# Two transformer blocks on one core: the ends of four stages computed in two halves of the positions

## What is computed

```python
mod = c_act @ mod_w[i] + mod_b[i]          # shifts, scales, gates; w_ada in block 2
y = mixer(rmsnorm(x, g_pre) * (1.0 + sc_m) + sh_m)    # ends in @ w2 (pw2), or @ w_out
x = x + gt_m * rmsnorm(y, g_post)          # "residual"
h = rmsnorm(x, g_pre_ffn) * (1.0 + sc_f) + sh_f       # "norm"
y = ffn(h)                                 # up products, gate, down products
x = x + gt_f * rmsnorm(y, g_post_ffn)
```

## Time and profile before

| | |
|---|---|
| median of 3 executions | 3444.75 us (3444.48 to 3445.12) |
| the profiled execution | 3445.46 us, span 3443.7 us |
| TensorE matmul busy | 3205.8 us, 93% |
| TensorE weight loads busy (beside the matmuls) | 2501.0 us, 73% |
| VectorE busy | 1513.4 us, 44% |
| ScalarE busy | 1024.8 us, 30% |
| GpSimd busy | 505.4 us, 15% |
| chain of work that ended last | PE 46%, DVE 4%, ACT 2%, DMA 1%, POOL 1% |
| mean granted TensorE clock | 0.954 |

### The profile page before, as it was taken

How to read it: one execution, slowest core, us unless ns; L and a number is a source line. 1 busy time by engine, 2 the same in 40 slices (tenths; PEclk the granted TensorE clock), 3 DMA queues, 4 the chain that set the end, 5 groups by cost and what they waited for, 6 DMA issues and landing times.

```text
span 3443.7 us, 33500 instructions
## 1 busy us (share of the span) xinstructions
PE 3205.8 (93%) x13818; PEld 2501.0 (73%) x13818; DVE 1513.4 (44%) x1620; ACT 1024.8 (30%) x1220; POOL 505.4 (15%) x210
## 2 busy tenths in 40 slices
PE   6897889999999999889999998899989999999996
PEld 1683456677888888668888877676666788888885
DVE  3777754353343344554521065577324422222225
ACT  2344435233222222233221132476222221111111
POOL 0397660100000000200200033000022000000002
PEclk8998998899999999979999999999999899999998
DMA  5113443302211211321332243531532121111112
GB/s 197 43 43 128 174 162 130 114 22 65 62 31 55 62 31 49 137 77 51 130 118 100 102 149 122 140 77 33 171 120 100 44 65 62 31 55 56 31 52 107
DMA packets 96191, 301.23 MB, mean 87 GB/s; under 512 B 11205, under 2 KB 15045, under 8 KB 95847
## 3 DMA queue, kind: packets, MB, share of 16 engines
q1 hardware_dynamic: 96040, 299.09, 26.5%
HBM read 251.34 MB, written 47.71 MB: 87 GB/s over the span
## 4 chain that ended last, share of the span: by engine, by line
PE 46%; DVE 4%; ACT 2%; issue 2%; DMA 1%; POOL 1%; SPq 0%; ACTq 0%; DVEq 0%; POOLq 0%
PE ps L651 38%; PE ps L697 2%; PE ps L988 2%; PE ps L1013 1%; PE ps L998 1%; DMA mainr<-sc_k 1%; PE ps L712 1%; DVE tmp L2044 1%; DVE tmp L2038 1%; POOL tmp L2277 1%; DVE tmp L2040 1%; DVE mainf L1672 1%; ACT mainr L1459 0%; PE ps L730 0%; DVE cols L2094 0%
## 5 line engine op out<-in xcount | busy, mean ns | idle before, releaser
L651 PE MATMUL ps<-mainr,wh 128*128 128x512 f32 (+1 forms) x7104 | 1939.9, 390 | 37.7 <-POOL wl L2205 11.6
L651 PEld LDWEIGHTS ps<-mainr,wh 128*128 128x128 f32 x7104 | 1337.4, 189 | 318.5 <-issue 40.9
L651 PE MATMUL ps<-mainr,wl 128*128 128x512 f32 (+1 forms) x3552 | 1131.5, 390 | 0.0
L651 PEld LDWEIGHTS ps<-mainr,wl 128*128 128x128 f32 x3552 | 671.8, 189 | 138.2
L1590 DVE TENSOR_TENSOR wl<-raw,wh 128x1024 fp32r<-128x1024 f32 (+2 forms) x256 | 271.1, 1063 | 630.2 <-ACT wh L1114 630.1
L1114 ACT CAST wh<-raw 128x1024 fp32r<-128x1024 f32 (+2 forms) x320 | 281.1, 886 | 749.5 <-PE ps L651 579.9
L2226 POOL TENSOR_TENSOR st<-st,tmp 128x1024 f32<-128x1024 f32 x24 | 57.5, 2396 | 1662.4 <-ACT tmp L1161 1662.1
L712 PE MATMUL ps<-raw,cols 128*1 128x512 f32 (+1 forms) x384 | 182.6, 632 | 43.7 <-DMA raw<-in_mod_w 18.3
L2205 POOL TENSOR_TENSOR wl<-raw,wh 128x1024 fp32r<-128x1024 f32 x64 | 154.3, 2419 | 456.0 <-ACT wh L1114 456.0
L697 PE MATMUL ps<-mainr,wh 128*128 128x512 f32 x576 | 164.6, 410 | 32.6 <-ACT mainr L1146 16.6
L1729 DVE TENSOR_TENSOR mainf<-mainf,ps 128x1024 f32<-128x1024 f32 x80 | 97.7, 1221 | 213.8 <-PE ps L651 213.0
(11 more groups left out here) (194 smaller groups left out, 2436.2 us busy)
## 6 DMA issues: line engine op xcount, KB each, us to landing
raw<-in_mod_w SPq DMA_DIRECT2D x48, 512.0 KB, 4.4
raw<-in_ada_w SPq DMA_DIRECT2D x48, 512.0 KB, 4.2
raw<-in_f_up SPq DMA_DIRECT2D x44, 512.0 KB, 3.5
raw<-in_g_up SPq DMA_DIRECT2D x44, 512.0 KB, 3.5
raw<-in_w_in SPq DMA_DIRECT2D x40, 512.0 KB, 4.1
raw<-in_pw SPq DMA_DIRECT2D x24, 512.0 KB, 3.8
sc_x<-mainf SPq DMA_DIRECT2D x24, 512.0 KB, 7.2
mainf<-sc_x SPq DMA_DIRECT2D x24, 512.0 KB, 7.5
```

What stands on the lines that cost most here:

```text
L651: ins = e.matmul(out, wt[:, a:b], xs[n], start=kk == 0 and t == 0, stop=kk == kt - 1 and t == 2)
```

## The change

The four ends are made in two halves of the positions, h = 0 (0 to 511) and h = 1. All eight tiles of the last product are made for half 0, then all eight for half 1. Each half has its own squares, four column sums (4 + 4 matmuls: all squares but the last are summed on GpSimd, then the last one apart), root, four diagonals, spread, residual and norm. While TensorE makes half 1's products, the other engines do half 0's residual and norm. Then the first three tiles of the next product are made in their half 0 and, after more of the end, in half 1.

- Weights: each weight of a last product is loaded and split twice, once per half (32 more loads, casts and low parts in all, half of them 512 wide). In the list, the next stage's first three weights now come before the eight pieces of modulation weights; before, they came behind them.
- PSUM: six half banks for the last products, one bank of statistics each for residual and norm; the temporaries are cut into ten halves.
- `tiles_abreast` takes the second and third tile one and three blocks behind the first, here and in the other two places that use it for full or half tiles (pw1, and the first tiles of pw2 and w_out).
- GpSimd: 6 adds of half width for each norm and half, 24 per end (12 in g's). Of g's residual it no longer does three adds.
- SP: the stores of x follow half 1's residual. The output is stored by halves.

The low part of a weight is now L1779 on VectorE, and a cast as before on ScalarE; columns L817, spread L824, modulation L772, turn L782, reciprocal L1848, diagonal L1854, residual L1863 and L1867, norm L1875, low part of it L1882, add of a last chunk L1929.

The core of the diff. Its pieces are, in this order: the table of what follows each end; the plan of an end (the list of weights, and the ring of half banks); TensorE's `tiles_abreast`, the end of pw2 and w_out (`project`), and that of f and g (`ffn_end`); the middle of ScalarE's `project`; VectorE's `project` and `ffn_end`; GpSimd's two. The functions they take the place of (`residual`, `square_columns`, `sums_added` and the like) are left out. `half_residual(s, i, h)` is a multiply and an add, `half_norm` and `half_lower` the norm's multiply and low part, `half_upper` its cast, `half_diagonal` a reciprocal and four diagonals.

```diff
...
+NEXT = {"pw2": ("n2", (3, 4), (("f_up", 0, 0), ("f_up", 0, 1), ("f_up", 1, 0))),
+        "f": ("n3", (5, 6), (("w_in", 0), ("w_in", 1), ("w_in", 2))),
+        "w_out": ("n4", (10, 11), (("g_up", 0, 0), ("g_up", 0, 1), ("g_up", 1, 0))),
+        "g": (None, (), ())}
...
+    def half_plan(self, s):
+
+        n, mods, first = NEXT[s]
+        for b in range(6):
+            self.bank.last[b] = self.acc.last[b // 2]
+        self.bank.only(*range(6))
+        for h in range(2):
+            for i in range(ND):
+                if s in ("f", "g"):
+                    key, src, done = (s + "_dn", LAST, i, h), self.d[f"{s}_dn{LAST}"][i], ("byadd", s, i, h)
+                else:
+                    key, src, done = (s, i, h), self.d[s][i], ("by", s, i, h)
+                self.weight(key, src, 128 * (len(CHUNKS[LAST]) if s in ("f", "g") else 8), "dve")
+                self.bank.take(key, done)
...
+        for key in first:
+            self.weight(key, self.d[key[0]][key[1] if len(key) == 2 else 2 * key[1] + key[2]], 1024, "dve")
+        for t, jb in enumerate(mods):
+            self.mod_weights("a", jb)
+            self.acc.put(2 - t, ("a", jb), *self.mod_free("a", jb))
...
+    def tiles_abreast(keys, kt, x, ready, outs, ends=True):
+
+        lags = (0, 1, 3)
+        for step in range(kt + lags[-1]):
+            for key, lag in zip(keys, lags):
+                kk, j = step - lag, k.W[key]
+                if not 0 <= kk < kt:
+                    continue
+                for event in ready(kk):
+                    w.wait_ge(*k.at(*event))
+                hi, lo = x(kk)
...
+        tiles_abreast([(s, i, 0) for i in range(3)], 8, part_of(x, 0), ready, lambda key: [k.BANK(*key)])
         for i in range(3, ND):
-            tile((s, i), 8, x, ready)
-        square_columns(s)
+            half_tile((s, i, 0), 8, x, ready, 0)
+        for i in range(ND):
+            half_tile((s, i, 1), 8, x, ready, 1)
+            if i == 0:
+                half_columns(s, 0)
+            if i == 1:
+                half_spread(s, 0)
+            if i == 5:
+                half_columns(n, 0)
+            if i == 6:
+                half_spread(n, 0)
+        modulation("a", mods[0], range(2))
+        half_columns(s, 1)
+        modulation("a", mods[0], range(2, 4))
+        half_spread(s, 1)
+        modulation("a", mods[1])
+        modulation_turn("a", mods[0])
+        first_tile(first[0], *following)
+        modulation_turn("a", mods[1])
+        half_columns(n, 1)
+        first_tile(first[1], *following)
+        half_spread(n, 1)
+        first_tile(first[2], *following)
+        x, ready = following
+        tiles_abreast(first, 8, part_of(x, 1), ready(1), lambda key: [k.ACC(*key)[:, 512:1024]])
...
+    def ffn_end(s, slots, following):
+
+        n, mods, first = NEXT[s]
+        fs = CHUNKS[LAST]
+        for h in range(2):
+            for i in range(ND):
+                half_tile((s + "_dn", LAST, i, h), len(fs), pairs(lambda kk: slots[0][fs[kk] % 5], lambda kk: slots[1][fs[kk] % 5]),
+                          lambda kk: [("uhi", s, fs[kk]), ("ulo", s, fs[kk])], h)
+                if (h, i) == (1, 1):
+                    half_columns(s, 0)
+                if (h, i) == (1, 2):
+                    half_spread(s, 0)
+        if not n:
+            half_columns(s, 1)
+            half_spread(s, 1)
+            return
+        modulation("a", mods[0])
+        half_columns(n, 0)
+        half_columns(s, 1)
+        modulation_turn("a", mods[0])
+        modulation("a", mods[1])
+        half_spread(n, 0)
+        half_spread(s, 1)
+        modulation_turn("a", mods[1])
+        x, ready = following
+        tiles_abreast(first, 8, part_of(x, 0), ready(0), lambda key: [k.ACC(*key)[:, 0:512]], ends=False)
+        half_columns(n, 1)
+        half_spread(n, 1)
+        tiles_abreast(first, 8, part_of(x, 1), ready(1), lambda key: [k.ACC(*key)[:, 512:1024]])
...
+        output(5, 1)
+        half_root(n, 0)
+        output(6, 1)
+        split_to(k.W[first[1]] + 1)
+        for i in range(7):
+            half_upper(n, i, 0, hi, shift, s, ND - 1)
+        output(7, 1)
+        split_to(k.W[first[2]] + 1)
+        half_upper(n, 7, 0, hi, shift, s, ND - 1)
...
+            split_to(k.W[s, i, 0] + 3)
+        split_to(k.W[s, 0, 1] + 3)
+        half_diagonal(s, 0)
...
+            half_residual(s, i, 0, y, x, x_load)
+            if i in (2, 5):
+                split_to(k.W[s, 1 + i // 3, 1] + 3)
+        split_to(k.W[s, 3, 1] + 3)
+        split_to(k.W[s, 4, 1] + 3)
+        half_diagonal(n, 0)
+        for i in range(ND):
+            half_norm(n, i, 0, x, s)
+            if i:
+                half_lower(n, i - 1, 0, hi, lo, shift, s, ND - 1)
+            if i in (1, 4):
+                split_to(k.W[first[i // 4]] + 1)
+        half_lower(n, ND - 1, 0, hi, lo, shift, s, ND - 1)
+        split_to(k.W[first[2]] + 1)
+        half_diagonal(s, 1)
+        for i in range(ND):
+            half_residual(s, i, 1, y, x, x_load)
...
+        def summed(i, h):
+            j = k.W[s + "_dn", LAST, i, h]
+            split_to(j + 3)
+            o = y(i)[:, 512 * h:512 * h + 512]
+            w.wait_ge(*k.at("tile", j))
+            w.wait_ge(*k.at("yadd", s, LAST - 1, i))
+            e.tensor_tensor(o, o, k.BANK(s + "_dn", LAST, i, h), ALU.add).then_inc(*k.to("byadd", s, i, h))
+
+        for i in range(ND):
+            summed(i, 0)
+        summed(0, 1)
+        summed(1, 1)
+        half_diagonal(s, 0)
+        summed(2, 1)
+        for i in range(ND):
+            half_residual(s, i, 0, y, x, x_load)
...
+        split_to(k.W[first[2]] + 1)
+        half_diagonal(n, 0)
+        half_diagonal(s, 1)
+        for i in range(ND):
+            half_norm(n, i, 0, x, s)
+            if i:
+                half_lower(n, i - 1, 0, hi, lo, shift, *last)
+            if i == 1:
+                modulation_add("a", mods[0])
+            if i == 4:
+                modulation_add("a", mods[1])
+        half_lower(n, ND - 1, 0, hi, lo, shift, *last)
+        for i in range(ND):
+            half_residual(s, i, 1, y, x, x_load)
...
+    def project(s):
+        n = NEXT[s][0]
+        squares_added(s, 0)
+        squares_added(s, 1, 1, 2)
+        squares_added(n, 0, 1, 3)
+        squares_added(s, 1, 2, 3)
+        squares_added(n, 0, 3, 7)
+        squares_added(s, 1, 3, 7)
+        squares_added(n, 1)
+
+    def ffn_end(s):
+        n = NEXT[s][0]
+        squares_added(s, 0)
+        squares_added(s, 1, 1, 3)
         for i in range(1, ND - 1):
-            w.wait_ge(*k.at("ysq", s, i))
-            if i > 1:
-                w.wait_ge(*k.at("yacc", s, i - 1))
-            e.tensor_tensor(k.S(0), k.S(0), k.TMP("ysq", s, i), ALU.add).then_inc(*k.to("yacc", s, i))
-
-    def sums_added(s):
-        for i in (1, 3, 5):
-            t = k.TMP("sum", s, i - 1)
-            w.wait_ge(*k.at("sumsq", s, i))
-            e.tensor_tensor(t, t, k.TMP("sum", s, i), ALU.add).then_inc(*k.to("sumadd", s, i))
+            if n:
+                squares_added(n, 0, i, i + 1)
+            if i + 2 < ND - 1:
+                squares_added(s, 1, i + 2, i + 3)
...
```

542 lines of the change are left out of this document (324 added, 218 removed).

## The result

The changed kernel takes 3454.24 us, the median of seven executions, against 3444.98 for the kernel before (3443.15 to 3446.5). One of the seven took 6466.14; the other six lie between 3450.6 and 3459.0, with a median of 3453.4. The ratio is 1.0026, 95% interval 1.0013 to 1.0038: slower by 9.3 us. The forecast was 3436, faster by 9. The time lies inside the range that was given, on the other side of no change.

A forecast was written before the change was run, and what follows sets the result against it. TensorE, busy 93% of the span, bounds the kernel; time can only come from its waits and non-product work. -10.3 + 2.7 - 11.9 - 2.0 + 13.1 - 4.0 + 3.2 = -9.2 gives 3436 us, range 3412 to 3458.

The forecast's parts named there:

- residual row of f's half 0 shared with GpSimd: At the f end: 4.6 us a row, 2.7 of it VectorE's own work, the rest for two GpSimd half adds.
- S: The moment in an end when TensorE starts the second half's products; later steps are timed from it.
- f end: End after f: half 0's chain outlasts half 1's products, 105.5 us against 92.4, so +13.1.
- weight (7,1) in pw2, w_out: At the pw2 and w_out ends: its low part stands behind half 0's norm, TensorE waits 5.0 us (2 to 8).
- g end: End after g: 51.4 us from S against 55.9 before, with a small allowance for GpSimd: -4.0 us.
- pw2 end: End after pw2: 58.7 us of work plus four waits and slow clock, 81.1 us against 91.4: -10.3.
- w_out: Its end 79.7 us against 91.6, -11.9; its start -2.0, as lags let more pieces run ahead of weight waits.
- Rival 3: At the ends GpSimd gets the port at every tie, residual rows of half 1 cost 2.6 us: 3456 us, chance 0.20.
- Rival 1: The f end comes out even because GpSimd's adds cost VectorE little: 3423 us, chance 0.17.
- Rival 2: At the ends only TensorE's own work counts, -30 us each, g -7.5: about 3345 us, chance 0.05.
- Rival 4: Even: the four waits near their upper ends in one of the pw2 and w_out ends, 3446 us, chance 0.13.
- The lags: At the starts of pw2 and w_out: pacing of the first three tiles changes, +2.7 us and -2.0 us.

The follow-up runs named there:

- experiment 2: The changed kernel with each load of x issued behind one weight of half 0, not all eight ahead of them, in all four ends: 3440.48 us.
- experiment 3: The changed kernel, but in f and g VectorE adds a half tile's product first and makes the low part behind it: 3450.80 us.
- experiment 4: The changed kernel with GpSimd's adds of squares cut to 8 of 512 columns, so the sums leave out most squares: 3428.85 us.
- experiment 6: The kernel before with only the lags of 0, 1 and 3 blocks in tiles_abreast, everything else as it was: 3420.49 us.
- kernel 1: The changed kernel, but the ring of three for high and low parts doesn't count an end's modulation weights, so the fourth weight takes the first tile's place: 3437.47 us.

## Why the prediction was right and wrong

**The step that failed** is one sentence: "The 32 more loads, casts and lower parts hide: ScalarE and VectorE are idle most of the product time". It was argued from idle engines. What counted was how long one weight lasts: 10.88 or 5.44 us of product before, 5.44 or 2.72 now, beside the queue ahead of it (the feed, 13.8 us in experiment 2) and the dependences from one weight to the next (the loop, 3.4 us in experiment 3). The sum had 0 for both, and the feed alone is enough to turn the sign: without it the kernel takes 3440.48, faster than before.

**The second, not in the sum at all,** is the place: the waits behind the third tile, 2.34, 0.91 and 2.94, of which the prediction says that each "stays". They became 5.05, 3.62 and 5.70, +8.2 us together by the rows, and 16.8 us when mended. The diff had it in view, the list of weights with the three ahead of the eight; I counted what that does to the loads, and not what it does to the ring that is indexed by the list.

**Term by term.**

| term | forecast | measured |
|---|---|---|
| residual row of f's half 0 shared with GpSimd | 4.6 | 4.55 |
| residual of f's half 0 ends, after S | 44.4 | 41.4 |
| third low part of w_in, after S | 47.3 | 44.3 |
| f end, from S | 127.3 | 122.8 |
| S in f, from the wait at the start of the chunk | 19.4 | 24.2 |
| weights (3,1), (4,1) in pw2 | 2 + 2 | 2.12 + 1.6 |
| weight (7,1) in pw2, w_out | 5.0 | 4.15, 4.05 |
| last modulation weight in pw2 | 2 | 2.51 |
| columns of half 1 in pw2 | 4 | 1.73 |
| g end: S, from the first product | 21.8 | 30.9 |
| g end from S | 51.4 | 53.8 |

The first row of the table is luck, as experiment 4 shows: GpSimd was taken at 1.9 us of a row and costs 0.67, and 1.21 is the wait for the cast that the sum left out.

The chain of the **f end** had the right owner, and its +13.1 came out as +13.5, but this is luck too, since several errors meet in it. S came 4.8 us late, which I put down to feed and loop without having taken it apart. From S on it was 4.5 shorter. The norm of half 0 began at S + 65.3, not 70. It took 11.1, not 14. The residual of half 1 took 12.8, not 15.5. What stands behind it took 33.7, not 27.8, and 2.8 of that is the longer wait of the place.

The **pw2 end**'s four waits were right in kind, three of them within 0.9 us; the stage is -1.2 and not -7.6, because of a feed wait of 3.32 and of 2.7 more behind the first tiles. **w_out** was -11.8 against -13.9, and the 2.7 more behind its first tiles would be enough for the difference. The **g end** was wrong in sign: its own chain was 2.4 longer than forecast, and S 9.1 late, by the wait of 4.63, the slow clock behind it, the loop, and a wait of 1.78 for the first half tile's input, which the kernel before does not have and which stays in experiment 2.

**The rivals.** Rival 3 said 3456 and named the port. The time is near its number by luck. Its mechanism was that a residual row of half 1 costs 2.6 us and not 1.94; in f three of these rows take 1.38 and five 1.71. GpSimd took less in the rows than the sum had for it, and it took something where the sum had nothing, in the half tiles of f and g. The place and the feed, 30.6 us when mended one by one, are none of the port; the loop, 3.4, is half of it. Rival 1 (the f end even) fell: the end was 13.5 longer. Rival 2 fell: TensorE's idle time rose. Rival 4 had the right sign of its errors and none of their causes. None of the rivals asked whether the weights keep up, which a halved tile should always raise.

**The Trainium skill's rule** on the port pair (SBUF — State Buffer, "Who interferes with whom": an exclusive lock, for a whole instruction) was right, and right that low parts can be hit too: 0.69 became 1.37 in g and 1.23 became 2.29 in pw2. This case's trace agrees nearly to the whole overlap. The low part at 3380.41 grew by 0.68 of the 0.82 us for which it lay beside GpSimd's add; the add at 1423.66 grew by 1.03 of 1.17; in the prediction's own 1.23 became 3.37, so 2.14 of 2.28. What is missing is 0.14 each time. What the prediction did not work out is that only the overlap with an add already running counts, so its price was too high where the two meet in part.

**The lags** were taken at +2.7 and -2.0 at the starts. Alone they are -24.5 (experiment 6). I had looked only at how they change the pace of the first tiles, not at whose buffer they free.

**Open.** Executions of kernel 1 scatter over 16 us (3426.1 to 3442.2). The fastest has the highest mean granted clock of the nine (0.963) and the slowest the lowest (0.959); only one of them is traced, and no run isolates the cause. What the 24.5 us of the lags hold beside the waits named is open. Not tried: f at full width with the other ends in halves, which the last table favours, and the sums of squares on TensorE in place of GpSimd.

## What to carry to other kernels

When tiles are cut in half and the weights stay whole, ask first how long one weight now lasts, and check every queue and every dependence between two weights against that; idle engines don't answer it. Where a list's order also decides a buffer's place, moving entries in the list moves places, and a consumer that lags makes its place the worst one to inherit: find out for each load which release it waits for. And time every small part of a change alone; here the smallest part was worth more than all the rest, and the whole hid it. A row that takes the time that was forecast is no proof of what it was forecast from: look at what fills it.

## What was unexpected of the hardware

When VectorE and GpSimd both work on two operands in SBUF, the one that begins later pays, whichever it is. Three rows of the changed kernel, in pw2's residual; alone, GpSimd's add takes 1.26 to 1.30, the low part 1.23:

```profile
621.70 0.69 DVE L1867 TENSOR_TENSOR mainf<-mainf,mainf 128x512 f32<-128x512 f32 x1
621.75 1.77 POOL L2504 TENSOR_TENSOR st<-st,tmp 128x512 f32<-128x512 f32 x1 [2.67 <-ACT tmp L1283]
622.31 2.29 DVE L1779 TENSOR_TENSOR wl<-raw,wh 128x1024 fp32r<-128x1024 f32 x1
```

GpSimd's add began 0.05 us behind VectorE's: the add of 0.69 kept its length, and GpSimd's grew by 0.48. The low part then began while that add ran, 1.21 us before its end, and grew by 1.06. In this trace 63 of VectorE's low parts (512 or 1024 columns) and residual adds begin while a GpSimd add of squares runs. Every one grows by the rest of that add less 0.14 or 0.15. Of the 84 GpSimd adds 46 begin beside such a VectorE operation and grow by its rest less 0.13 to 0.17; the other 38 take 1.26 to 1.30. VectorE's multiply L1863, one of whose operands lies in PSUM, pays nothing: 29 of them lie beside a GpSimd add and take 0.73 to 0.75, as the others do. The page's group of the 84 adds has the mean, 1527 ns:

```profile
L2504 POOL TENSOR_TENSOR st<-st,tmp 128x512 f32<-128x512 f32 x84 | 127.9, 1527 | 1750.7 <-ACT tmp L1283 1747.8
```

And a wait of 5 us costs more than its length: behind 5.05 the four matmuls took 2.05 us, behind 0.98 in experiment 1 they took 1.17. After the 3.62 at g_up they took 1.17 as well.
